# Rotary turns of a mixed-layer transformer block: the exchange of halves moves from a TensorE product to small DMAs

## The chip, the cores and the metric

The kernel runs on one core of a Trainium2 chip, as one program. The metric is the device time of one execution in microseconds (us), the median of three runs. The profile is of one execution, with the span from its first to its last instruction.

## The reference, cut to what matters

A sequence of 256 tokens with 1024 features goes through two stacks. The first has two layers, each a feed-forward network, a mixer and another feed-forward network. Mixer 0 has delta-rule heads and retention heads; mixer 1 has differential and dilated attention. The second stack has two more layers, each with block attention (8 heads of 64), a gated recurrence (hgrn, 4 heads) and attention to a memory. Queries and keys of retention, differential, dilated and block attention get a rotary turn:

```
x1, x2 = halves of the rotated dims
out = concat([x1 * cos - x2 * sin, x2 * cos + x1 * sin])
```

The halves are 32 of 64 dims for retention and differential attention, 64 of 128 for dilated attention. In block attention only the first 16 of 64 dims turn (8 and 8), and its queries and keys are normalised over 64 dims first.

## The kernel before, in words

Features lie on the partitions and tokens on the free axis, so that a half of a head is a range of partitions. A unit of rotary work is a 128-partition, 2-block, 256-token piece (128x512 f32). There are 18 units: `r64` 0 and 1 in mixer 0; `r64b` 0 to 3 and `r128` 0 to 3 in mixer 1; `mq0`, `mk0`, `mq1`, `mk1` (0 and 1 of each) in the two last mixers. All that multiplies weights is cut into panels of 1024 KB, loaded by SyncE's queue into three slots (`raw`), split by ScalarE into a high part (`w_hi`, L1571, in halves L1580) and by VectorE into a low part (`w_lo`, L1890, in halves L1873), and multiplied by TensorE in three products (L1060 to L1062). A panel can be multiplied as two halves.

The order of every engine is written out by hand as one list, `ORDER`, and each engine takes its own steps of it in that order. Lists of rounds are merged, and `weave` puts half panels between the rounds (`BESIDE_0`, `BESIDE_1`, `BESIDE_2`). Waits are on counted steps of other engines (`at(...)`).

One rotary unit is two steps:

```
swap (pe):  ps[:, bank] = matrix^T @ values          # L1454, a signed permutation, fp32
rope (dve): tmp = ps[:, bank] * sin                  # L2130
            values = values * cos                    # L2131
            values = values + tmp                    # L2132
```

Both are of the same round (`ROPE = [("pe","swap",0), ("dve","rope",0)]`). Around them:

- Mixer 0: the `beside` lists of `delta_rounds` hold the two swaps next to the doubling of a triangular inverse (`double_y`, `double`, `turn_again` on TensorE, L1317; `doubled` on VectorE, L2084; `corner` on GpSimd, L1029). `ret_scores` (L1428) waits for the second rope.
- Mixer 1: the four `r64b` units lie between panels 4 to 7 of `in1`; the four `r128` units, two per round, lie in the first two rounds of the attention heads. A head is `scores` (TensorE, L1478 and L1480), `mask_max` (VectorE, L2180), `exp` (ScalarE, L1784), `divide` (VectorE, L2193 to L2201), `turn_p` (TensorE, L1490), `p_cols` (ScalarE, L1795), `attend` (TensorE, L1433).
- Last mixers: after the last of eight `level` rounds of the recurrence (`k_level` on GpSimd, L1037), one normalisation per round: `cn_sq` (ScalarE), `cn_sum` (TensorE, L1465), `cn_rstd` (ScalarE, L1773 and L1774), `cn_use` (VectorE, L2144; for the `ho` units L2146, L2148, L2136, L2137), in the order mq 0, mk 0, mq 1, mk 1, ho 0, ho 1. The swap and rope of unit i lie in the round after its `cn_use`; a half panel lies in every round. Block attention starts seven rounds after the last level.

GpSimd has little to do: loads of tables (L1017), `add` (L1044), `corner`, `k_level`, and the four stores of the output (L1049).

Of the kernel before, what the change touches and what calls it, by code (L numbers as in the profile page):

```python
# [82 lines left out]
def tables():  # L83
# [6 lines left out]

    def swap(n, half, signs=True, width=None):

        m = np.zeros((P, P), f)
        for g in range(0, P, n):
            for d in range(half):
                m[g + d + half, g + d] = -1.0
                m[g + d, g + d + half] = 1.0
        return m

    def rope(dim):  # L100
        inv = (np.float32(10000.0) ** (-np.arange(0, dim, 2, dtype=f) / f(dim))).astype(f)
        ang = (np.arange(SEQ, dtype=f)[None, :] * inv[:, None]).astype(f)
        reps = P // (dim // 2)
        return np.tile(np.cos(ang), (reps, 1)).astype(f), np.tile(np.sin(ang), (reps, 1)).astype(f)

# [28 lines left out]
    for g in (0, 64):  # L134
        freq[g:g + half, 0] = inv2
        freq[g + half:g + 2 * half, 0] = inv2
# [3 lines left out]
        [("upper", upper), ("strict", strict_low), ("diag16", diag16), ("e16", below(16)), ("e32", below(32)),  # L140
         ("e64", below(64)), ("ret", np.concatenate(ret, axis=1)), ("cos64", cos64), ("sin64", sin64),
         ("swap64", swap(64, 32))],
        [("causal", causal), ("times", times), ("union", union), ("cos64", cos64), ("sin64", sin64),
         ("swap64", swap(64, 32)), ("cos128", cos128), ("sin128", sin128), ("swap128", swap(128, 64))],
        [("causal", causal), ("swapp", swap(64, 8)), ("levels", np.concatenate(levels, axis=1)),
         ("keep", keep), ("freq", freq)],
# [21 lines left out]
LATE = {name: (BASE[name] + N_OF[name] + SLOTS - 1, min(BASE[name] + N_OF[name] + SLOTS, PANELS)) for name in DOWNS}  # L168
UNCOUNTED = {"out_part", "half", "half_hi", "half_lo", "gate_first", "up_first", "first_hi", "first_lo", "ffn_down", "logs", "split_hi", "split_lo", "ffn", "panel", "load", "store"}
PAIRS = DC // 2  # L170
# [64 lines left out]
SCORES_FIRST = [ATTEND[1], ATTEND[0]] + ATTEND_TWO[2:]  # L235
ROPE = [("pe", "swap", 0), ("dve", "rope", 0)]
NORM_ROPE = NORM_COLS + [("pe", "swap", 2), ("dve", "rope", 2)]

# [107 lines left out]
def delta_rounds():  # L346
# [10 lines left out]
    for s in range(3):  # L357
        doubling += [both(("pe", "double_y", s), *([("pe", "turn_again", s)] if s else []), ("act", "y", s), *([("act", "t_again", s)] if s else [])),
                     both(("pe", "double", s), ("dve", "doubled", s), *([("pool", "corner", s + 1)] if s < 2 else []))]
    beside = [[("pe", "turn_v", (0,)), ("pe", "turn_v", (1,)), ("dve", "v_beta", (0,)), ("dve", "v_beta", (1,))],  # L360
              [("pe", "turn_k", ()), ("dve", "k_decayed", ()), ("pe", "swap", (("r64", 0),)), ("dve", "rope", (("r64", 0),))],
              [("pe", "swap", (("r64", 1),)), ("dve", "q_decayed", ()), ("dve", "rope", (("r64", 1),))],
              [(e, k, (h,)) for h in (0, 1) for e, k in (("pe", "ret_scores"), ("dve", "ret_decay"))],
# [61 lines left out]
def last_mixer(l):  # L425

    hgrn, ahead = hgrn_rounds(l)
    hgrn[ahead + 9] += [("act", "silu", (f"in2_{l}", 15)), ("act", "logs", ())]
    n = ahead + 9
    qk = [(f"mq{l}", 0), (f"mk{l}", 0), (f"mq{l}", 1), (f"mk{l}", 1)]  # L430
    h = n + 7
    chains = [hgrn,
              [[]] * n + rounds(NORM_COLS, qk + [(f"ho{l}", 0), (f"ho{l}", 1)]),
              [[]] * (n + 2) + rounds(ROPE, qk),
              [[]] * h + paired_heads(l),
              [[]] * (h + 6) + [[("dve", "gate_out", ((f"moba{l}", 0),))], [], [], [("dve", "gate_out", ((f"moba{l}", 1),))]],
              [[]] * (h + 13) + [y_splits(l, 0), y_splits(l, 2)]]
    if l == 0:
        load, *stats = mem_norm(1)
        chains += [[[]] * (h + 1) + [[load]]]  # L440
    if l:
        chains += [[[]] * (h + 7) + sum(([[("pe", "turn_back", (b,)), ("act", "rows_back", (b,))], []] for b in range(PAIRS)), [])]
    places = [n + r for r in BESIDE_2]
    if l:
        places[:4] = [0, 1, 2, 2]
    panels = panel_list(f"in2_{l}", None, 4)
    panels[-1] = [x for x in panels[-1] if x[1] != "evacuate"]
    out = weave(merge(*chains), halves(panels), places)
    return (out + late_splits(f"in2_{l}") + [("dve", "gate_out", ((f"matt{l}", g),)) for g in (0, 1)]
            + y_splits(l, 8) + y_splits(l, 10))  # L450
# [36 lines left out]
def order():  # L487
# [37 lines left out]
    out += weave(rounds(ROPE, [("r64b", g) for g in (0, 2, 1, 3)]), panel_list("in1", None, 4, 8), range(4))  # L525
    ropes = [[(e, k, (("r128", g),)) for g in pair for e, k, _ in ROPE] for pair in ((0, 2), (1, 3))]
    heads = rounds(SCORES_FIRST, [("dif", h) for h in range(4)] + [("dil", h) for h in range(4)])
# [56 lines left out]
def build(nc, x_in, mem_in, pos_in, panels, gains, small_in, tab0, tab1, tab2, tab3, out):  # L584
    with ExitStack() as ctx:
# [159 lines left out]
        def evac(name, k):  # L745
            return ("dve" if (name, k) in EVACUATED_BY_DVE else "act", "evacuate", name, k)

        ropes = {}
        for g in range(2):
            ropes["r64", g] = (rqk[:, 2 * g:2 * g + 2], tab(1, "swap64"), tab(1, "cos64"), tab(1, "sin64"), 3 - g, evac("in0", 11))  # L750
        for g in range(4):
            ropes["r128", g] = (cqk[:, 2 * g:2 * g + 2], tab(2, "swap128"), tab(2, "cos128"), tab(2, "sin128"), 6 + g // 2,
                                evac("in1", 4 + g))
            ropes["r64b", g] = (dqk[:, 2 * g:2 * g + 2], tab(2, "swap64"), tab(2, "cos64"), tab(2, "sin64"), 6 + g // 2,
                                evac("in1", g))
            for l in range(2):
                unit_ = ((f"mq{l}", f"mk{l}")[g // 2], g % 2)
                ropes[unit_] = (mo_qk[:, 2 * g:2 * g + 2], tab(3, "swapp"), cos_a, sin_a, 2 + g // 2, ("dve", "cn_use", unit_))
        rope_list = [a for e, k, a in ORDER if k == "swap"]
        rope_index = {a[0]: i for i, a in enumerate(rope_list)}  # L760

# [175 lines left out]
        last_use["mem0"] = ("dve", "cn_use", ("ro", 1))  # L937
        last_use["mem1"] = ("dve", "cn_use", ("ho0", 1))

# [70 lines left out]
        def _(pool):  # L1010
# [20 lines left out]
            def k_level(l, v):  # L1031
# [5 lines left out]
                nc.gpsimd.tensor_tensor(k_l[v % 2], k_g, dec_f[v % 2], ALU.mult).then_inc(pool_done, 1)  # L1037

            def add(tag, b):

# [11 lines left out]

            steps("pool", {"load": load, "add": add, "zero": zero, "corner": corner, "k_level": k_level, "store": store})


        @block.tensor
        def _(pe):
# [383 lines left out]

            def swap(unit):
                values, matrix, _, _, bank, ready = ropes[unit]
                pe.wait_ge(done[ready[0]], at(*ready))
                if rope_index[unit] >= 2:
                    pe.wait_ge(dve_done, at("dve", "rope", rope_list[rope_index[unit] - 2][0]))
                for t_ in ("tab1", "tab2", "tab3"):
                    if unit[0] in {"tab1": ("r64",), "tab2": ("r128", "r64b"), "tab3": ("mq0", "mk0", "mq1", "mk1")}[t_]:
                        pe.wait_ge(loaded[t_], 16)
                if unit[0] == "r64b":  # L1450
                    pe.wait_ge(dve_done, at("dve", "ropes_scaled"))
                if unit[0] == "r64":
                    pe.wait_ge(dve_done, at("dve", "k_decayed") if unit[1] else at("dve", "v_beta", 1))
                pe.matmul(ps[:, bank], matrix, values, start=True, stop=True).then_inc(pe_done, 1)  # L1454

            def cn_sum(unit):
# [79 lines left out]
            def hgrn_out(l, g):  # L1536
                pe.wait_ge(dve_done, at("dve", "level_in", l, 7))
                for i in range(2):
# [11 lines left out]
                         "from_state": from_state, "delta_out": delta_out, "ret_scores": ret_scores, "ret_out": ret_out,  # L1550
                         "swap": swap, "cn_sum": cn_sum, "scores": scores, "turn_p": turn_p, "attend": attend,
                         "lam_sum": lam_sum, "diagonal": diagonal, "level": level, "hgrn_out": hgrn_out})
# [291 lines left out]
        def _(dve):  # L1844
# [279 lines left out]
            def rope(unit):  # L2124
                values, _, cos, sin, bank, _ = ropes[unit]
                dve.wait_ge(pe_done, at("pe", "swap", unit))
                if unit[0][0] == "m":
                    dve.wait_ge(act_done, at("act", "sines"))
                tmp = grid(xn[:, 512:1024], 2)
                step(tt(tmp, grid(ps[:, bank], 2), spread(sin, 2), ALU.mult))  # L2130
                step(tt(values, values, spread(cos, 2), ALU.mult))  # L2131
                finish(tt(values, values, tmp, ALU.add))  # L2132
# [264 lines left out]
```

## Time and profile before

| | |
|---|---|
| time, median of 3 runs | 1557.71 us (1556.43 to 1557.83) |
| profiled execution: span | 1554.0 us |
| profiled execution: mean granted TensorE clock | 0.997 |
| TensorE busy | 1499.8 us, 97% |
| VectorE busy | 1171.7 us, 75% |
| ScalarE busy | 763.9 us, 49% |
| GpSimd busy | 94.1 us, 6% |
| DMA, mean | 159 GB/s, 246.76 MB |

The page gives the span of the profiled execution and no other time for it. The three runs took 2.4 to 3.8 us more than this span, the median 3.7 us more; a change of the span is taken as a change of the time. The busy shares are averages over stages that have different limits.

### The profile page before, as it was taken

How to read it: one execution, taken by the hardware profiler on the slowest of the kernel's cores; microseconds unless marked ns; L12 is line 12 of the kernel's file. 1: busy time of each engine (PE TensorE's matmuls, PEld its weight loads, DVE VectorE, ACT ScalarE, POOL GpSimd, SP SyncE). 2: the span in 40 equal slices, each digit the busy share in tenths (PEclk: the TensorE clock that was granted, in tenths of full speed). 3: DMA queues.
4: the chain of work that ended last, by engine and by line, in shares of the span. 5: the costliest groups of instructions: out<-in, count | busy, mean ns of one | idle time of the engine just before them, and what ended most of it. 6: DMA issues, size and time to landing. Idle time of an engine off the chain costs nothing.

```text
span 1554.0 us, 23910 instructions
## 1 busy us (share of the span) xinstructions
PE 1499.8 (97%) x9958; PEld 1343.8 (86%) x9958; DVE 1171.7 (75%) x1387; ACT 763.9 (49%) x935; POOL 94.1 (6%) x66
## 2 busy tenths in 40 slices
PE   7999999999999999999998899999999989999988
PEld 6888899988888888888887888888899869899967
DVE  7878668756887788787676688787779676579774
ACT  5333456445433453334445543345565675564662
POOL 2000010011000010000100100001113001003100
PEclk9999999999999999999999999999999999999999
DMA  7555535214655555555441365554344315444302
GB/s 272 209 190 189 170 131 188 82 55 159 213 189 199 179 178 190 190 185 194 163 163 56 134 216 190 192 188 175 151 163 152 109 42 189 175 149 152 120 28 81
DMA packets 51888, 246.76 MB, mean 159 GB/s; under 512 B 4619, under 2 KB 5771, under 8 KB 27718
## 3 DMA queue, kind: packets, MB, share of 16 engines
q1 hardware_dynamic: 50662, 238.29, 43.8%
q0 software_dynamic: 1120, 6.96, 1.2%
q8 instruction: 79, 1.29, 0.3%
q14 instruction: 27, 0.22, 0.0%
HBM read 244.18 MB, written 1.05 MB: 158 GB/s over the span
## 4 chain that ended last, share of the span: by engine, by line
PE 76%; DVE 13%; ACT 7%; issue 3%; DMA 0%; SPq 0%; DVEq 0%; ACTq 0%; POOL 0%
PE ps L1109 20%; PE ps L1111 10%; PE ps L1060 9%; PE ps L1062 9%; PE ps L1061 9%; PE ps L1162 8%; PE ps L1317 4%; PE ps L1163 4%; DVE w_lo L1890 3%; ACT w_hi L1571 2%; DVE act_two L1998 1%; PE ps L1465 1%; ACT work L1784 1%; ACT act_two L1649 1%; PE ps L1454 1%
## 5 line engine op out<-in xcount | busy, mean ns | idle before, releaser
L1571 ACT ACTIVATE w_hi<-raw 128x2048 fp32r<-128x2048 f32 x186 | 355.2, 1914 | 396.6 <-PE ps L1111 276.6
L1890 DVE TENSOR_TENSOR w_lo<-raw,w_hi 128x2048 fp32r<-128x2048 f32 x186 | 432.4, 2331 | 139.1 <-ACT w_hi L1571 136.3
L1109 PE MATMUL ps<-act_two,w_hi 128*128 128x512 f32 x1408 | 445.1, 398 | 5.0 <-DVE w_lo L1890 2.4
L1060 PE MATMUL ps<-act_two,w_hi 128*128 128x256 f32 x1120 | 329.0, 294 | 9.9 <-DVE act_two L1998 5.3
L1111 PEld LDWEIGHTS ps<-act_two,w_lo 128*128 128x128 f32 x1408 | 265.6, 189 | 63.1
L1061 PE MATMUL ps<-act_two,w_hi 128*128 128x256 f32 x1120 | 316.7, 283 | 0.0
L1062 PE MATMUL ps<-act_two,w_lo 128*128 128x256 f32 x1120 | 316.7, 283 | 0.0
L1111 PE MATMUL ps<-act_two,w_lo 128*128 128x256 f32 x1408 | 277.5, 279 | 0.0
L1060 PEld LDWEIGHTS ps<-act_two,w_hi 128*128 128x128 f32 x1120 | 214.6, 192 | 17.0 <-issue 6.1
L1109 PEld LDWEIGHTS ps<-act_two,w_hi 128*128 128x128 f32 x1408 | 215.5, 190 | 8.0 <-DVE w_lo L1890 3.6
L1061 PEld LDWEIGHTS ps<-act_two,w_hi 128*128 128x128 f32 x1120 | 214.7, 192 | 4.4 <-issue 4.3
L1062 PEld LDWEIGHTS ps<-act_two,w_lo 128*128 128x128 f32 x1120 | 214.5, 192 | 0.0
L1162 PE MATMUL ps<-g_two,w_hi 128*128 128x512 f32 x384 | 135.7, 396 | 0.0
L1873 DVE TENSOR_TENSOR w_lo<-raw,w_hi 128x1024 fp32r<-128x1024 f32 x76 | 103.5, 1388 | 27.4 <-ACT w_hi L1580 26.1
L1162 PE MATMUL ps<-act_two,w_hi 128*128 128x512 f32 x320 | 113.0, 397 | 2.5 <-DVE act_two L1929 2.5
L1163 PE MATMUL ps<-g_two,w_lo 128*128 128x256 f32 x384 | 107.2, 279 | 0.0
L1060 PE MATMUL ps<-w_hi,act_two 128*128 128x256 f32 (+1 forms) x336 | 105.0, 312 | 0.2 <-ACT work L1668 0.2
L1061 PE MATMUL ps<-w_lo,act_two 128*128 128x256 f32 (+1 forms) x336 | 100.1, 298 | 0.0
L1062 PE MATMUL ps<-w_hi,act_two 128*128 128x256 f32 (+1 forms) x336 | 100.1, 298 | 0.0
L1044 POOL TENSOR_TENSOR pair<-pair 128x512 f32<-128x512 f32 x27 | 41.2, 1526 | 858.7 <-ACT pair L1628 857.9
L1163 PE MATMUL ps<-act_two,w_lo 128*128 128x256 f32 x320 | 89.3, 279 | 0.0
L1162 PEld LDWEIGHTS ps<-g_two,w_hi 128*128 128x128 f32 x384 | 72.1, 188 | 16.7
(286 smaller groups left out, 1995.5 us busy)
## 6 DMA issues: line engine op xcount, KB each, us to landing
raw<-panels SPq DMA_DIRECT2D x184, 1024.0 KB, 4.8
raw<-panels SPq DMA_DIRECT2D x80, 512.0 KB, 4.9
raw<-panels SPq DMA_DIRECT2D x8, 256.0 KB, 5.7
table<-tab POOLq DMA_DIRECT2D x1, 1472.0 KB, 9.4
table<-tab POOLq DMA_DIRECT2D x1, 1216.0 KB, 5.5
xn<-x_in SPq DMA_DIRECT2D x4, 256.0 KB, 4.9
work<-mem_in POOLq DMA_DIRECT2D x1, 1024.0 KB, 9.3
xn<-mem_in POOLq DMA_DIRECT2D x1, 1024.0 KB, 6.3
```

Source lines behind the costliest of these rows:

```text
L1044: nc.gpsimd.tensor_tensor(pair[:, 0:512], pair[:, 0:512], pair[:, 512 * b:512 * b + 512], ALU.add).then_inc(pool_done, 1)
L1060: pe.matmul(o, l[0], r[0], start=start, stop=False, skip_group_check=shared)
L1061: pe.matmul(o, l[0], r[1], start=False, stop=False, skip_group_check=shared)
L1062: return pe.matmul(o, l[1], r[0], start=False, stop=stop, skip_group_check=shared)
L1109: pe.matmul(grid(ps[:, bank + half], 2), w[half][0], act_two[:, slots[c]], start=c == 0, stop=False)
L1111: ins = pe.matmul(ps[:, bank + half, 0:SEQ], w[half][1], act_hi[:, slots[c]], start=False, stop=c == DC - 1)
L1162: pe.matmul(grid(ps[:, bank], 2), hi, two, start=first and m == 0, stop=False)
L1163: ins = pe.matmul(ps[:, bank, 0:SEQ], lo, two[:, 0], start=False, stop=last and m == len(quarters) - 1)
L1317: ins = pe.transpose(oh, lhs(h), ident) if turn else pe.matmul(oh, lhs(h), rhs(h), start=True, stop=True)
L1571: nc.scalar.activation(w_hi[:, s], raw[:, s], ACT.Copy).then_inc(panel_hi, 1)
L1873: ins = tt(w_lo[:, s, c], raw[:, s, c], w_hi[:, s, c].bitcast(F32), ALU.subtract)
L1890: tt(w_lo[:, s], raw[:, s], w_hi[:, s].bitcast(F32), ALU.subtract).then_inc(panel_lo, 1)
```

## The change

The permutation product goes. In its place GpSimd's queue issues DMAs that copy, inside SBUF, each half of a head to the partitions of the other half, into a new buffer `other` (free parts of `work`). The sign goes into the sine table, whose first half of each head is negated; for block attention the frequency of the first 8 dims is negated. A unit of 64-wide heads takes 4 DMAs (of 32 partitions with 2 KB each, or of 8 partitions for block attention), a unit of 128-wide heads takes 2 of 64 partitions: 8 + 16 + 8 + 32 = 64 DMAs in all. Each unit has its own semaphore, and `rope` waits for all its DMAs. `rope` comes one round after the exchange in `ROPE`. In mixer 0 the exchanges are listed two rounds ahead at most, and the ropes stay where they were. In the first two rounds of the heads of mixer 1, all four `r128` exchanges are listed in the first round and the ropes in the second and third. In each last mixer a new step `still` zeroes the 128x2048 buffer, because only 16 of 64 rows per head are ever written there. The load of the second memory waits for the last rope.

```diff
-ROPE = [("pe", "swap", 0), ("dve", "rope", 0)]
+ROPE = [("pool", "swap", 0), ("dve", "rope", 1)]

 # delta_rounds
-    beside = [[("pe", "turn_v", (0,)), ("pe", "turn_v", (1,)), ("dve", "v_beta", (0,)), ("dve", "v_beta", (1,))],
-              [("pe", "turn_k", ()), ("dve", "k_decayed", ()), ("pe", "swap", (("r64", 0),)), ("dve", "rope", (("r64", 0),))],
-              [("pe", "swap", (("r64", 1),)), ("dve", "q_decayed", ()), ("dve", "rope", (("r64", 1),))],
+    beside = [[("pool", "swap", (("r64", 0),)), ("pool", "swap", (("r64", 1),)), ("pe", "turn_v", (0,)), ("pe", "turn_v", (1,)), ("dve", "v_beta", (0,)), ("dve", "v_beta", (1,))],
+              [("pe", "turn_k", ()), ("dve", "k_decayed", ()), ("dve", "rope", (("r64", 0),))],
+              [("dve", "q_decayed", ()), ("dve", "rope", (("r64", 1),))],

 # last_mixer
-              [[]] * (n + 2) + rounds(ROPE, qk),
+              [[]] * (n + 1) + [[("pool", "still", (l,))]] + rounds(ROPE, qk),

 # order
-    ropes = [[(e, k, (("r128", g),)) for g in pair for e, k, _ in ROPE] for pair in ((0, 2), (1, 3))]
+    ropes = [[("pool", "swap", (("r128", g),)) for g in (0, 2, 1, 3)]] + [[("dve", "rope", (("r128", g),)) for g in pair] for pair in ((0, 2), (1, 3))]

-        last_use["mem1"] = ("dve", "cn_use", ("ho0", 1))
+        last_use["mem1"] = ("dve", "rope", ("mk0", 1))

+            def still(l):
+                pool.wait_ge(pe_done, at("pe", "level", l, 7))
+                nc.gpsimd.memset(work[:, 5120:7168], 0.0).then_inc(pool_done, 1)
+
+            def swap(unit):
+                values, to, _, _, (n, half), ready = ropes[unit]
+                pool.wait_ge(done[ready[0]], at(*ready))
+                if unit[0] == "r64":
+                    pool.wait_ge(pe_done, at("pe", "pow8", 1))
+                if unit[0] == "r128":
+                    pool.wait_ge(dve_done, at("dve", "rope", ("r64b", unit[1])))
+                if unit[0][0] == "m":
+                    pool.wait_ge(pool_done, at("pool", "still", int(unit[0][2])))
+                for a in range(0, P, n):
+                    pool.dma_start(to[a:a + half], values[a + half:a + 2 * half]).then_inc(swapped[unit], 16)
+                    pool.dma_start(to[a + half:a + 2 * half], values[a:a + half]).then_inc(swapped[unit], 16)

             def rope(unit):
-                dve.wait_ge(pe_done, at("pe", "swap", unit))
+                dve.wait_ge(swapped[unit], 32 * P // n)
+                if unit[0] == "r64":
+                    dve.wait_ge(loaded["tab1"], 16)
...
-                step(tt(tmp, grid(ps[:, bank], 2), spread(sin, 2), ALU.mult))
+                step(tt(tmp, other_, spread(sin, 2), ALU.mult))
```

Here `ready` is the step that wrote the values: an evacuation, or `cn_use` in the last mixers. TensorE's `swap`, with its waits for bank use, for tables and for `ropes_scaled`, is removed, and the three permutation matrices leave the tables.

## Rows read from the trace of the kernel before

**Rows 1.** The page: TensorE's busy time, and the shares of the last chain.
```profile
PE 1499.8 (97%) x9958; PEld 1343.8 (86%) x9958; DVE 1171.7 (75%) x1387; ACT 763.9 (49%) x935; POOL 94.1 (6%) x66
...
PE 76%; DVE 13%; ACT 7%; issue 3%; DMA 0%; SPq 0%; DVEq 0%; ACTq 0%; POOL 0%
```

**Rows 2.** Groups by line of TensorE: busy us, mean ns, idle before.
```profile
L1454 PE MATMUL ps<-work,table 128*128 128x512 f32 x36 | 18.1, 594 | 0.4 <-DVE table L1992 0.4
```

**Rows 3.** The chain in mixer 0: start us, us.
```profile
317.27 0.86 PE ps L1454 x2
...
319.92 0.86 PE ps L1454 x2
```

**Rows 4.** Timeline of TensorE in mixer 0: start us, us, engine, line, operation.
```profile
304.09 1.06 PE L1317 MATMUL ps<-work,xn 128*128 128x128 f32 x8
...
326.24 0.71 PE L1428 MATMUL ps<-work 64*128 64x256 f32 x4
```

**Rows 5.** Timeline of VectorE in mixer 0.
```profile
324.03 0.69 DVE L2132 TENSOR_TENSOR work<-work,xn 128x512 f32<-128x512 f32 x1
```

**Rows 6.** Timeline of GpSimd, mixer 0 and the first of two last mixers.
```profile
316.09 2.50 POOL L1029 TENSOR_TENSOR work<-work,table 128x512 f32<-128x512 f32 x2 [13.08 <-PE ps L1317]
...
1196.48 2.43 POOL L1037 TENSOR_TENSOR xn<-work,pair 128x1024 f32<-128x1024 f32 x1 [5.12 <-ACT work L1671]
```

**Rows 7.** Timeline of VectorE: pairs of half-panel splits in two places.
```profile
351.50 2.36 DVE L1873 TENSOR_TENSOR w_lo<-raw,w_hi 128x1024 fp32r<-128x1024 f32 x2
...
1197.86 3.27 DVE L1873 TENSOR_TENSOR w_lo<-raw,w_hi 128x1024 fp32r<-128x1024 f32 x2
```

**Rows 8.** Timeline of TensorE in mixer 1.
```profile
798.71 1.02 PE L1454 MATMUL ps<-work,table 128*128 128x512 f32 x2
...
805.31 1.88 PE L1454 MATMUL ps<-work,table 128*128 128x512 f32 x4
...
828.86 0.50 PE L1478 MATMUL ps<-work 64*128 64x128 f32 x4 [1.47 <-DVE stat L2180]
```

**Rows 9.** The chain in mixer 1.
```profile
807.94 2.29 DVE w_lo L1890
...
819.35 0.70 DVE work L2132
...
821.31 1.88 ACT work L1784 x8
...
827.52 0.28 DVE work L2180
```

**Rows 10.** Timeline of TensorE in the first of the two last mixers.
```profile
1228.91 1.02 PE L1465 MATMUL ps<-pair,const 128*128 128x512 f32 x2
```

**Rows 11.** Timeline of VectorE in the same mixer.
```profile
1223.05 0.75 DVE L2144 SCALAR_TENSOR_TENSOR work<-work,small,pair 128x512 f32<-128x512 f32 x1 [3.34 <-ACT pair L1774]
...
1231.36 0.75 DVE L2144 SCALAR_TENSOR_TENSOR work<-work,small,pair 128x512 f32<-128x512 f32 x1 [0.40 <-ACT pair L1774]
...
1235.95 0.75 DVE L2144 SCALAR_TENSOR_TENSOR work<-work,small,pair 128x512 f32<-128x512 f32 x1 [0.40 <-ACT pair L1774]
```

**Rows 12.** The chain in the same mixer.
```profile
1240.54 0.76 DVE xn L2146
...
1247.39 0.70 DVE act_two L2137
```

**Rows 13.** Timeline of GpSimd: one of the four stores.
```profile
1548.76 0.54 POOL L1049 DMA_DIRECT2D out<-work  x1 [0.82 <-DVE work L1964]
```

**Rows 14.** The page, DMA issues: count, KB each, median us to landing.
```profile
table<-tab POOLq DMA_DIRECT2D x1, 1472.0 KB, 9.4
...
out<-work POOLq DMA_DIRECT2D x4, 256.0 KB, 2.5
```

**Rows 15.** Stretches of mixer 1: us, busy us (x count) of PE, PEld, DVE, ACT, POOL; clock; DMA.
```profile
850.00:852.00 2.00, 0.79 (x4) 0.55 (x4) 1.90 (x11) 1.56 (x6) 0.00 (x0) 1.00 0.04 8
...
854.00:856.00 2.00, 2.00 (x3) 0.76 (x3) 0.00 (x0) 0.30 (x1) 0.00 (x0) 0.51 0.00 0
```

More of the change, by code:

```diff
@@ L89, in tables @@
     strict_low = (part > free).astype(f)
[L91 to L98, printed above, removed]
     def rope(dim):
@@ L102, in rope @@
         ang = (np.arange(SEQ, dtype=f)[None, :] * inv[:, None]).astype(f)
-        reps = P // (dim // 2)
-        return np.tile(np.cos(ang), (reps, 1)).astype(f), np.tile(np.sin(ang), (reps, 1)).astype(f)
+        reps = P // dim
+        return np.tile(np.cos(ang), (2 * reps, 1)).astype(f), np.tile(np.concatenate([-np.sin(ang), np.sin(ang)]), (reps, 1)).astype(f)
     q0 = part - free
@@ L134, in tables @@
     for g in (0, 64):
-        freq[g:g + half, 0] = inv2
+        freq[g:g + half, 0] = -inv2
         freq[g + half:g + 2 * half, 0] = inv2
@@ L140, in tables @@
         [("upper", upper), ("strict", strict_low), ("diag16", diag16), ("e16", below(16)), ("e32", below(32)),
-         ("e64", below(64)), ("ret", np.concatenate(ret, axis=1)), ("cos64", cos64), ("sin64", sin64),
-         ("swap64", swap(64, 32))],
+         ("e64", below(64)), ("ret", np.concatenate(ret, axis=1)), ("cos64", cos64), ("sin64", sin64)],
         [("causal", causal), ("times", times), ("union", union), ("cos64", cos64), ("sin64", sin64),
-         ("swap64", swap(64, 32)), ("cos128", cos128), ("sin128", sin128), ("swap128", swap(128, 64))],
-        [("causal", causal), ("swapp", swap(64, 8)), ("levels", np.concatenate(levels, axis=1)),
+         ("cos128", cos128), ("sin128", sin128)],
+        [("causal", causal), ("levels", np.concatenate(levels, axis=1)),
          ("keep", keep), ("freq", freq)],
@@ L168 @@
 LATE = {name: (BASE[name] + N_OF[name] + SLOTS - 1, min(BASE[name] + N_OF[name] + SLOTS, PANELS)) for name in DOWNS}
-UNCOUNTED = {"out_part", "half", "half_hi", "half_lo", "gate_first", "up_first", "first_hi", "first_lo", "ffn_down", "logs", "split_hi", "split_lo", "ffn", "panel", "load", "store"}
+UNCOUNTED = {"swap", "out_part", "half", "half_hi", "half_lo", "gate_first", "up_first", "first_hi", "first_lo", "ffn_down", "logs", "split_hi", "split_lo", "ffn", "panel", "load", "store"}
 PAIRS = DC // 2
@@ L746, in evac @@
             return ("dve" if (name, k) in EVACUATED_BY_DVE else "act", "evacuate", name, k)
+        other = [region(1024 + 512 * i, 2, SEQ) for i in range(2)]
+        other_1 = [region(13312 + 512 * i, 2, SEQ) for i in range(4)]
+        other_2 = [region(5120 + 512 * i, 2, SEQ) for i in range(4)]
         ropes = {}
         for g in range(2):
-            ropes["r64", g] = (rqk[:, 2 * g:2 * g + 2], tab(1, "swap64"), tab(1, "cos64"), tab(1, "sin64"), 3 - g, evac("in0", 11))
+            ropes["r64", g] = (rqk[:, 2 * g:2 * g + 2], other[g], tab(1, "cos64"), tab(1, "sin64"), (64, 32), evac("in0", 11))
         for g in range(4):
[L752 to L755, printed above, removed]
+            ropes["r64b", g] = (dqk[:, 2 * g:2 * g + 2], other_1[g], tab(2, "cos64"), tab(2, "sin64"), (64, 32), evac("in1", g))
+            ropes["r128", g] = (cqk[:, 2 * g:2 * g + 2], other_1[g], tab(2, "cos128"), tab(2, "sin128"), (128, 64), evac("in1", 4 + g))
             for l in range(2):
                 unit_ = ((f"mq{l}", f"mk{l}")[g // 2], g % 2)
-                ropes[unit_] = (mo_qk[:, 2 * g:2 * g + 2], tab(3, "swapp"), cos_a, sin_a, 2 + g // 2, ("dve", "cn_use", unit_))
-        rope_list = [a for e, k, a in ORDER if k == "swap"]
-        rope_index = {a[0]: i for i, a in enumerate(rope_list)}
+                ropes[unit_] = (mo_qk[:, 2 * g:2 * g + 2], other_2[g], cos_a, sin_a, (64, 8), ("dve", "cn_use", unit_))
+        swapped = {u: sem("swapped_" + u[0] + f"_{u[1]}") for u in ropes}
         def bank_of(name, k):
@@ L1051, in store @@
                     pool.wait_ge(stored, 16 * TILES * 2)
-            steps("pool", {"load": load, "add": add, "zero": zero, "corner": corner, "k_level": k_level, "store": store})
+            steps("pool", {"load": load, "add": add, "still": still, "swap": swap, "zero": zero, "corner": corner, "k_level": k_level, "store": store})
         @block.tensor
@@ L1440, in ret_out @@
                          ret_p[h][:, 0:SEQ], ret_p[h][:, SEQ:384]).then_inc(pe_done, 1)
[L1442 to L1454, printed above, removed]
             def cn_sum(unit):
@@ L1550, in _ @@
                          "from_state": from_state, "delta_out": delta_out, "ret_scores": ret_scores, "ret_out": ret_out,
-                         "swap": swap, "cn_sum": cn_sum, "scores": scores, "turn_p": turn_p, "attend": attend,
+                         "cn_sum": cn_sum, "scores": scores, "turn_p": turn_p, "attend": attend,
                          "lam_sum": lam_sum, "diagonal": diagonal, "level": level, "hgrn_out": hgrn_out})
@@ L2124, in rope @@
             def rope(unit):
-                values, _, cos, sin, bank, _ = ropes[unit]
-                dve.wait_ge(pe_done, at("pe", "swap", unit))
+                values, other_, cos, sin, (n, _), _ = ropes[unit]
+                dve.wait_ge(swapped[unit], 32 * P // n)
+                if unit[0] == "r64":
+                    dve.wait_ge(loaded["tab1"], 16)
                 if unit[0][0] == "m":
```

1 line of the change is left out of this document (removed).

## The prediction

> **What bounds the kernel now.** I read the page first: TensorE is busy 97% of the span and the last chain runs on it for three quarters [rows 1]. So work taken off TensorE should count, but only where the chain is really there. Therefore I read, stage by stage, the groups by line for the price of the product, the chain in the four places with rotary units, and then the timelines of TensorE, VectorE and GpSimd, to see who is ready first once the product is gone. A difference of under 0.2% (3.1 us) can't be told from none here.
>
> The 18 products are 36 records [rows 2]; one product occupies TensorE and the chain for 0.86 us [rows 3]. All 18 together are 18 x 0.86 = 15.5 us. That is the most this change can give. I now go through the places and ask what is left of it.
>
> **Mixer 0 (2 units).** Both products are on the chain [rows 3], 1.72 us. The exchanges may be issued when TensorE has finished the records that end at 305.15 [rows 4], far ahead of the first rope at 318.1, and GpSimd is free until its corners at 316.09 [rows 6]. One issue of GpSimd takes 0.54 us [rows 13]; eight take 4.3 us and end at 309.5. The landing is not shown for such copies: the lower bound is the store's 2.5 us, the upper one the table's 9.4 us [rows 14]. Even the upper gives 309.0 + 9.4 = 318.4 for the second unit, which is needed only after 322. I price the exchange at nothing here; it is covered by the inverse's rounds. Now VectorE is late next. The retention scores start at 326.24 [rows 4] and would start at 324.5, but they wait for the second rope, whose last instruction ended at 324.72 [rows 5]. The rope no longer waits for its product, 0.15 us earlier. Against this, its first multiply will read two SBUF operands at 318.1, while GpSimd's corner runs from SBUF until 318.59 [rows 6]. The trace shows what that does: a pair of half splits takes 3.27 us where GpSimd's k_level overlaps it and 2.36 us elsewhere [rows 6, 7]. So the multiply starts at 318.6, the second rope ends at 325.1, and the scores start 1.1 us earlier than before instead of 1.72. Bounds: -1.6 (no blocking) and -1.1. I take -1.1, since the row shows the blocking. Taken on its own, "SBUF — State Buffer" (Who interferes with whom) in the Trainium skill says the same: a VectorE instruction with two SBUF inputs waits for a GpSimd one that reads SBUF, and does not wait for one that only writes. By this rule the new zeroing of the buffer would block nothing, and mixer 0 keeps the 1.1.
>
> **Mixer 1 (8 units).** The first four products lie between full panels, where TensorE is the chain: 4 x 0.86 = 3.44, plus the 0.4 us wait for the scaled tables before the first [rows 2], is 3.9 us. The exchanges of these units can all go as soon as their panels are evacuated, a panel or more ahead; covered. From 805.31 the other four products [rows 8] come. But the chain leaves TensorE there: the split of 807.94, two pairs of ropes with a mask_max behind each, then ScalarE's exp, a split, and the next mask_max at 827.52 [rows 9]. TensorE waits 1.47 us for VectorE at 828.86 [rows 8]. After the change VectorE's order is split, mask_max, ropes, mask_max, then exp and the splits on both engines, then the second pair of ropes, then the third mask_max. These are the same pieces in series; only their order differs. So the four products at 805 and 813 give nothing back, and the stage keeps 3.9 us. The r128 exchanges are issued from about 796 and the last at 803, against ropes at 807.5 and 819: covered even by 9.4 us.
>
> **Last mixers (4 units each).** Before, a round was 4.59 us: a sum, a product and a half panel on TensorE. VectorE's work in it (cn_use, rope, half split) is 4.59 - 0.40 = 4.19 us [rows 11]. Take the product out and TensorE's round is 3.73 us, shorter than VectorE's: VectorE becomes the bound. Walk it through with the rope one round later:
> - The cn_use of mq 1 comes 2.45 us after the start of its sum [rows 10, 11]. One product fewer stands before it: 1231.36 - 0.86 = 1230.50. Its round now has the rope of mq 0: until 1230.50 + 4.22 = 1234.72.
> - The next cn_use is ready at 1235.95 - 1.72 = 1234.23, so VectorE is already the later one: until 1238.94.
> - The cn_use of ho 0 was at 1240.54 and is ready at 1240.54 - 2.58 = 1237.96; it starts at 1238.94, 1.6 us earlier than before.
> - Before, VectorE then did cn_use, one rope, cn_use, until 1248.1 [rows 12], 7.58 us. Now there are two ropes in this tail, because of the lag. A rope is three instructions of 0.69 [rows 5], with gaps 2.18 us. So 1238.94 + 7.58 + 2.18 = 1248.7.
> - The first mask_max of block attention stands behind that on VectorE, and exp, divide and turn_p behind mask_max. It is 0.6 us later than before, though TensorE arrives 3.4 us earlier.
>
> So each last mixer costs 0.6 us instead of giving 3.4. The second has the same rounds. The zeroing starts at 1215 and must be done by 1223.8, when the first exchange is ready: a 128x1024 product takes GpSimd 2.43 us [rows 6], so twice that, 4.9, is my upper bound and 0 the lower; covered by 8.8 us. What waits behind the exchanges on GpSimd is the load of the second memory, 0.6 us later, needed some 30 us on.
>
> The exchange itself has less cover here. The one of mq 0 is issued from 1223.80 [rows 11]; the fourth DMA starts 3 x 0.54 = 1.6 us later; VectorE comes for it at 1230.50 + 0.78 = 1231.3. The landing may thus take 5.9 us before it costs anything; the other three have more. Bounds: 1.6 + 2.5 (no wait) and 1.6 + 9.4 = 11.0 us (3.5 us wait in each mixer). I take the store's 2.5 us: its 256 KB from SBUF by the same queue is nearer to 16 KB pieces than a 1472 KB table. A page alone has a price for this: by "DMA: Bandwidth & Descriptors" (Anatomy of one DMA) of the Trainium skill a small DMA of this path takes about 2.0 us, most of it the receipt of the write; an estimate with it would leave the sum as it is.
>
> **The sum.** -1.1 - 3.9 + 0.6 + 0.6 = -3.8 us. The span 1554.0 becomes 1550.2. The median of the runs stands 3.7 us above the span, so 1553.9 us. The extra traffic is 3.1 MB of 247; I leave it out.
>
> **Rivals.**
> - *Everything given to TensorE is kept.* Speaks for it: 97% busy. Against: the chain is on VectorE in the heads and in the tails [rows 9, 12]. It would give 1557.7 - 15.5 = 1542.2.
> - *Late landings.* If a copy lands late because it shares the engines with panel loads, VectorE stands at the first rope of each last mixer. At 9.4 us it costs 3.5 each: 1560.9; halfway, 1557.4. For it: the only heavily mixed row. Against: its size.
> - *The clock falls.* In mixer 1, VectorE's share does not shrink, so TensorE will wait in one piece: its work from 801.4 ends near 819, the next scores come at 828.86 - 3.9 = 825, 6 us idle. In the last mixers it would stand 3 us before the scores of the second pair. The trace has one fall, to half (1.2 GHz), after a stretch in which TensorE was busy 0.8 us of 2 [rows 15]; sums on the chain took twice 0.86 there and attention products 0.43 more, 1.3 us in all. Three such falls on the chain take back 3.9: 1557.8. Against: in mixer 1 the slowed half panel has slack. In the Trainium skill, "TensorE: Matmul & The Clock Gate" (The HAM clock gate) states that idling halves the clock; by this rule it would fall, and the trace agrees that it can.
> - *Slower: the software queue takes the copies one after another.* Place: the last mixers, where 16 DMAs are issued from 1223.8 and the last must be there by 1246.5. It decides from 1.63 us per DMA (26.2 us for 16, 3.5 us late in each mixer, over 3.1 us slower in all). At 2.5 us each, 40 us: 17.3 late twice and 2.3 in mixer 0, about 1591. Against: the stores were issued 1.4 us apart, each landing after 2.5, so two were under way together [rows 13, 14].
>
> **How the numbers follow.** Forecast 0.54, with 1551.5 to 1556.5 as its own range (a clock fall more or less is 1.3 each way, mixer 0 up to 0.5). Everything kept 0.05, late landings 0.17, clock 0.15, one after another 0.09. The range 1550.5 to 1560.5 leaves out the first and the last of the rivals and the tips of the others. Faster: three quarters of 0.54, the 0.05, and 0.04 of the middle ones, 0.50. Slower: 0.09 and 0.04 of late landings, 0.13. Same: 0.37.
>
> **What would show it.** Mixer 0: retention scores about 1.1 us closer to the last corner, and the first rope's multiply longer than 0.69. Mixer 1: panels 4 to 7 at 5.75 us each, then an idle TensorE of some 6 us before the scores of the fourth head. Last mixers: half panels every 3.73 us, VectorE without idle time from the third cn_use on, and TensorE idle before the second pair of scores. I am wrong if ropes wait for DMAs, if an issue takes GpSimd much more than 0.54 us, or if VectorE's instructions are longer while GpSimd issues.

## The result and the profile after

| | before | after |
|---|---|---|
| time, median of 5 runs each (of before, the three runs above and two more) | 1556.43 us (1555.55 to 1557.83) | 1561.79 us (1560.98 to 1563.57) |
| span of the profiled execution | 1554.0 us | 1561.0 us |
| mean granted TensorE clock | 0.997 | 0.987 |

Ratio after to before 1.0034, 95% interval 1.0023 to 1.0045: the change makes the kernel 5.4 us slower. The forecast was 1553.9 us, with 1560.5 as the upper end of its range; it gave 0.13 to a kernel that is slower by more than 3.1 us.

To find where the time went I took marks, that is instructions of GpSimd that stand in both traces: the first corner of mixer 0, the load of the next table that ends a mixer, the first and last `add` of a norm, the load of the second memory, the stores. The table gives how much the distance between two marks grew, after minus before, in us:

| stage | forecast | measured |
|---|---|---|
| start, to the first `add` | 0 | +1.5 |
| mixer 0 (first corner to table load) | -1.1 | +2.25 |
| mixer 1 | -3.9 | -3.60 |
| last mixer 1 | +0.6 | +0.96 |
| last mixer 2 | +0.6 | +0.83 |
| last store's issue to the end of the span | 0 | +4.98 |

The stretches between these stages changed by 0.1 us in all. The start stands before any changed instruction; in the profiles of this study it lies between 16.8 and 19.1 us with and without the exchange, and the profiled execution is the slowest of the five. I leave it out. The other rows add up to +5.4 us, the difference of the medians. That they agree so closely is in part luck, since mixer 1 alone differs by 1.4 us between profiles of the same work (spare_counters, below).

**Mixer 0.** Timeline of TensorE after (start us, us); it answers to the scores of [rows 4]:

```profile
325.59 0.60 PE L1325 MATMUL ps<-const,work 128*128 128x128 f32 x4
328.50 0.83 PE L1436 MATMUL ps<-work 64*128 64x256 f32 x4 [2.31 <-DVE work L2128]
329.10 0.65 PE L1437 MATMUL ps<-work 64*128 64x128 f32 x4
329.69 3.32 PE L1325 MATMUL ps<-work,xn 128*128 128x128 f32 x16
```

TensorE stands 2.31 us in front of the retention scores, for the last instruction of the second rope. Timelines of VectorE and of GpSimd in the same place, against [rows 5, 6]:

```profile
318.98 0.69 DVE L2060 TENSOR_TENSOR work<-ps,stat 128x512 f32<-128x512 f32 x1 [4.19 <-PE ps L1325]
319.70 1.04 DVE L2126 TENSOR_TENSOR xn<-work,table 128x512 f32<-128x512 f32 x1
...
324.40 0.69 DVE L2126 TENSOR_TENSOR xn<-work,table 128x512 f32<-128x512 f32 x1
325.13 1.65 DVE L2127 TENSOR_TENSOR work<-work,table 128x512 f32<-128x512 f32 x1
326.81 1.63 DVE L2128 TENSOR_TENSOR work<-work,xn 128x512 f32<-128x512 f32 x1
```

```profile
317.70 2.50 POOL L1018 TENSOR_TENSOR work<-work,table 128x512 f32<-128x512 f32 x2 [6.33 <-PE ps L1325]
...
324.57 3.33 POOL L1018 TENSOR_TENSOR work<-work,table 128x512 f32<-128x512 f32 x2 [4.37 <-PE ps L1325]
```

Two instructions of the second rope take 1.65 and 1.63 us instead of 0.69 while the second pair of corners (324.57 to 327.90) runs on GpSimd. Beside the first pair it is the same: the rope's first multiply, with two SBUF operands, takes 1.04, while the one at 318.98, which reads PSUM, takes its usual 0.69. The second pair before, on GpSimd's timeline:

```profile
324.69 2.60 POOL L1029 TENSOR_TENSOR work<-work,table 128x512 f32<-128x512 f32 x2 [6.10 <-PE ps L1317]
```

It took 2.60 us, now 3.33, and it began just as the second rope ended at 324.72 [rows 5]. The stage begins 1.60 us later in the profile after. Measured from its start, TensorE delivers the pair's inputs 1.72 us sooner, with both products gone, while VectorE comes to the second rope 0.22 us later (324.40 against 322.58), so that the two now meet.

The wait has a tail. Stretches of the same time (us; busy us of PE, PEld, DVE, ACT, POOL; granted clock; DMA):

```profile
326.00:328.00 2.00, 0.19 (x2) 0.00 (x0) 1.97 (x2) 0.88 (x2) 1.90 (x2) 1.00 0.00 0
...
330.00:332.00 2.00, 2.00 (x11) 2.00 (x11) 1.09 (x3) 0.00 (x0) 0.00 (x0) 0.50 0.00 0
```

After the idle stretch the granted clock is 0.50, the lower level of 1.2 GHz. From the first score (328.50) to the next panel piece (333.79) TensorE takes 5.29 us for what took 3.70 before (326.24 to 329.94), 1.6 us more. "TensorE: Matmul & The Clock Gate" (The HAM clock gate) in the Trainium skill says that idling lowers the clock; the trace agrees. Sum: two products -1.72; without them the scores were due at 326.24 + 1.60 (shift of the stage) - 1.72 = 326.12 and came at 328.50, +2.38; the slow clock +1.59; together +2.25.

**Mixer 1.** Timeline of TensorE after, against 828.86 of [rows 8]:

```profile
828.73 0.59 PE L1472 MATMUL ps<-work 64*128 64x128 f32 x2 [5.63 <-DVE stat L2176]
```

This is the forecast's picture: TensorE is done early and waits some 6 us for the `mask_max` behind the second pair of ropes.

**Last mixers.** The chain after in the first of them, against [rows 12]:

```profile
1224.72 0.86 PE ps L1459 x2
...
1228.45 0.87 PE ps L1459 x2
...
1230.73 0.76 DVE work L2140
...
1234.84 0.75 DVE work L2140
...
1239.02 0.67 DVE xn L2142
...
1241.63 0.70 DVE xn L2126
...
1243.81 0.76 DVE xn L2142
...
1246.51 0.70 DVE xn L2126
...
1248.98 0.34 DVE work L2176
```

TensorE's rounds are 3.73 us, VectorE's 4.1 to 4.2, and two ropes stand in the tail, as walked through. The chain names no DMA. Before, the same `mask_max` stood in the chain at

```profile
1248.41 0.34 DVE work L2180
```

Less the 0.25 us by which this stage begins later, it is 0.32 us later. The other 0.64 us come behind it. Among them is a wait of VectorE for a product of TensorE, 0.43 us in front of the `mask_max` at 1253.48, where before (1252.56) there was none. The stretches there:

```profile
1247.00:1249.00 2.00, 0.00 (x0) 0.00 (x0) 1.90 (x6) 0.00 (x0) 0.06 (x1) 1.00 0.00 0
...
1251.00:1253.00 2.00, 1.82 (x7) 1.00 (x6) 1.56 (x8) 1.79 (x5) 0.00 (x0) 0.50 0.93 393
```

The second of them before, with the clock at its upper level:

```profile
1251.00:1253.00 2.00, 0.99 (x7) 0.52 (x6) 1.79 (x10) 1.91 (x4) 0.00 (x0) 1.00 0.93 381
```

**The exchanges themselves** are cheap. From the list of DMA issues (KB each, median us to landing) and the timeline of GpSimd (one issue):

```profile
work<-work POOLq DMA_DIRECT2D x24, 64.0 KB, 2.3
...
work<-work POOLq DMA_DIRECT2D x8, 128.0 KB, 3.7
...
work<-work POOLq DMA_DIRECT2D x32, 16.0 KB, 1.9
```

```profile
308.92 0.50 POOL L1045 DMA_DIRECT2D work<-work  x1
```

**The end.** The last store, before and after, on GpSimd's timeline:

```profile
1550.12 0.54 POOL L1049 DMA_DIRECT2D out<-work  x1 [0.82 <-DVE work L1964]
...
1552.14 0.54 POOL L1057 DMA_DIRECT2D out<-work  x1 [0.82 <-DVE work L1958]
```

The last store is issued 2.02 us later than before, but the span ends 8.9 us behind it (1561.0) instead of 3.9 (1554.0). The stores land no later. No engine shows an instruction there. TensorE stands still, and from about 1555 us on its granted clock is 0.50, so that a part of the lower mean clock in the table above is this idle end and costs nothing.

### The profile page after: what moved, and what is told of

Read it like the earlier page. It is cut to its first block, busy times and chain, and to the rows that moved or that the text cites. A ratio compares the mean times of both kernels' runs of the same rounds, so it can differ in the third digit from the quotient of the medians.

```text
span 1561.0 us, 23895 instructions
## 1 busy us (share of the span) xinstructions
PE 1495.5 (96%) x9922; PEld 1345.7 (86%) x9922; DVE 1173.4 (75%) x1387; ACT 764.5 (49%) x935; POOL 130.5 (8%) x132
## 4 chain that ended last, share of the span: by engine, by line
PE 75%; DVE 15%; ACT 6%; issue 2%; DMA 0%; SPq 0%; DVEq 0%; POOL 0%; ACTq 0%
PE ps L1117 20%; PE ps L1119 10%; PE ps L1068 9%; PE ps L1070 9%; PE ps L1069 9%; PE ps L1170 8%; PE ps L1171 4%; PE ps L1325 4%; DVE w_lo L1884 3%; ACT w_hi L1565 2%; DVE act_two L1992 1%; PE ps L1459 1%; ACT act_two L1643 1%; DVE w_lo L1867 1%; DVE work L2127 1%
```

## The experiments

Each kernel below is the changed kernel or the kernel before with the edit that is shown, cut to the lines that matter. Theory 1: in mixer 0 a collision of VectorE and GpSimd makes TensorE wait and the clock fall. For the end (the stretch from the last store's issue to the end of the span, 3.9 us before) there were two theories: A, each further semaphore lengthens it; B, each DMA of GpSimd's software queue does. Times are medians, ratios are to the kernel before in the same series, with 95% intervals. Its median was 1557.1 us for the first four kernels, 1556.8 for the next four, 1555.4 for the last two.

### m0_early: mixer 0's ropes where VectorE is idle

```
-  ... ("dve", "v_beta", (1,))],
-  [("pe", "turn_k", ()), ("dve", "k_decayed", ()), ("dve", "rope", (("r64", 0),))],
-  [("dve", "q_decayed", ()), ("dve", "rope", (("r64", 1),))],
+  ... ("dve", "v_beta", (1,)), ("dve", "rope", (("r64", 0),)), ("dve", "rope", (("r64", 1),))],
+  [("pe", "turn_k", ()), ("dve", "k_decayed", ())],
+  [("dve", "q_decayed", ())],
```

> The changed kernel with one thing moved: VectorE does both ropes of mixer 0 right behind v_beta, where it stood idle from 314.8 to 318.98 after the change, instead of after k_decayed and q_decayed. Theory 1 (the second rope collides with GpSimd's corner at 324.57, TensorE then waits 2.3 us and the clock falls to half for 3.4 us, 1.7 us lost): the retention scores no longer wait for a rope, no fall of the clock at 328, the stage from the first corner's inputs to the end of mixer 0 is 2.3 + 1.7 = 4.0 us shorter than in the changed kernel, the time about 1557.8. Rival (the exchange's DMAs are what makes the stage longer, by slowing others or by landing late): the stage changes by less than 1 us, about 1561.5.

Measured: 1557.63 us, ratio 1.0004 (0.9995 to 1.0012), 4.2 us below the changed kernel as the same series has it (1561.82, four_counters). Mixer 0 is 1.71 us shorter than before, 3.96 us shorter than in the changed kernel. Its VectorE timeline shows that the collision has only moved, to the first pair of corners, which start at 315.50:

```profile
315.54 1.78 DVE L2128 TENSOR_TENSOR work<-work,table 128x512 f32<-128x512 f32 x1
317.36 1.64 DVE L2129 TENSOR_TENSOR work<-work,xn 128x512 f32<-128x512 f32 x1
```

There it costs nothing: the rope ends at 319.0, TensorE needs it at 324, and the granted clock stays 1.00:

```profile
328.00:330.00 2.00, 2.00 (x20) 2.00 (x18) 0.90 (x2) 0.00 (x0) 0.00 (x0) 1.00 0.00 0
```

Theory 1 stands. The wait and the fall of the clock went together, so this run gives their sum and the timeline above how it divides. The rival of theory 1, that the exchange's own DMAs make mixer 0 longer, falls: they are all there.

### four_counters: 4 semaphores instead of 18

```
-swapped = {u: sem("swapped_" + u[0] + f"_{u[1]}") for u in ropes}
+slots = [sem(f"swapped_{i}") for i in range(4)]      # counted up from place to place
...
-dve.wait_ge(swapped[unit], 32 * P // n)
+dve.wait_ge(swapped[unit], full[unit])
```

> The changed kernel with 4 semaphores for the landings of the exchanges, counted up from place to place, instead of 18; the same 64 DMAs. The end of the changed kernel, from the last store's issue to the end of the span, is 8.9 us against 3.9 before. Theory A (each further semaphore lengthens the end, 5.0 / 18 = 0.28 us each): the end becomes 3.9 + 4 x 0.28 = 5.0 us and the time falls by 3 to 4 us, to about 1558. Theory B (the use of GpSimd's software queue, 64 more DMAs, lengthens the end): it stays at 8.9 us, and the time at 1561.8.

Measured: 1561.82 us, ratio 1.0028 (1.0018 to 1.0038); the end is 8.9 us. Against theory A.

### spare_counters: 18 idle semaphores in the kernel before

```
+spare = [sem(f"spare_{i}") for i in range(18)]
```

> The kernel before with 18 more semaphores that nothing uses, no exchange at all. Theory A, if it is their mere number that counts at the end: the end of the span 5.0 us longer, the time about 1556.4 + 4 = 1560. Theory B, or if only used ones count: no change, 1556.4.

Measured: 1556.20 us, ratio 0.9996 (0.9987 to 1.0005); the end is 3.8 us. Theory A is out. The profile is also a measure of noise: with the same work, mixer 1 is 1.4 us shorter and the stretch behind it 2.3 us longer than in the profile of before. The stretches show what goes with it. In the profile of before the granted clock falls at 852 to 856 us [rows 15], 14 us ahead of the end of mixer 1; here it stays 1.00 until 858 and falls at 858 to 862, 4 us ahead of that end. All profiles divide so. With the products mixer 1 takes 114.1 or 114.2 us where a fall lies at this earlier place (before, small_copies) and 112.65 where it does not (spare_counters). With the exchange it takes 110.2 to 110.5 us with the earlier fall (after, four_counters, mixer1_sync_queue, products_in_last, all_sync) and 108.7 with a later one or none (m0_early, early_lag0, only_mixer1, mixed_queues). Like against like, the exchange makes mixer 1 3.6 to 4.0 us shorter.

### only_mixer1: the exchange in mixer 1 alone

```
+by_product = ("r64", "mq0", "mk0", "mq1", "mk1")
...
+if unit[0] in by_product:
+    dve.wait_ge(pe_done, at("pe", "half_turn", unit))   # the product of before
+    other_ = grid(ps[:, turn[unit][2]], 2)
```

> The exchange in mixer 1 alone (8 units, 24 DMAs, 8 semaphores); mixer 0 and the last mixers keep the permutation product on TensorE and the order of before. Mixer 1 gives back 3.6 us as in the changed kernel, the other stages are those of before. By theory A the end costs 8 x 0.28 = 2.2 us of span: 1556.4 - 3.6 + 2 = about 1555. By theory B it costs 5.0 x 24/64 = 1.9 if it goes with the number of DMAs, or the whole if one is enough: 1555 to 1558. If the gain of mixer 1 hung on the other places it would be 1556.4 or more.

Measured: 1553.94 us, ratio 0.9979 (0.9970 to 0.9988): 3.1 us below before. In its profile mixer 0 and the last mixers are those of before within 0.04 us, and the end is 1.76 us longer for 24 DMAs. So mixer 1 gives 3.1 + 1.8 = 4.9 us; with the interval's 1.4 us to either side this agrees with the 3.9 forecast, and it does so without the other places. The profile by itself has mixer 1 5.42 us shorter than before and the stretch behind it 2.31 us longer; against spare_counters, whose fall of the clock comes late too, the two are 3.98 us shorter and 0.03 us longer.

### small_copies: 64 copies that nobody needs, in the kernel before

```
 pool.dma_start(to, of_).then_inc(loaded[tag], 16)
+if tag == "tab1":
+    for i in range(64):
+        pool.dma_start(scrap[...], const[...]).then_inc(small_copies, 16)     # 32 partitions x 64 bytes
```

> The kernel before, with all its products, and 64 small copies (32 partitions x 64 bytes) issued on GpSimd's queue right behind the first table's load at 24 us, into a tile that nothing reads; GpSimd is idle there until 194 us. Theory B (each software DMA, whenever it is issued, lengthens the end of the program): the last stage's times stay, the end of the span after the last store's issue goes from 3.9 to 8.9 us, the time from 1557.1 to about 1561. Rival: the longer end comes from something else in the changed kernel (semaphores are already out), then the end stays 3.9 us and the time 1557.1.

Measured: 1561.89 us, ratio 1.0033 (1.0021 to 1.0046), as slow as the changed kernel. The copies are issued here, where GpSimd is idle:

```profile
25.41 31.59 POOL L1022 DMA_DIRECT2D scrap<-const  x64
```

The mixers are unchanged, all within 0.1 us. The last store and the span:

```profile
1549.82 0.54 POOL L1054 DMA_DIRECT2D out<-work  x1 [0.82 <-DVE work L1970]
```

```profile
span 1559.0 us, 23976 instructions
```

From the store to the end it is 9.2 us, 5.3 more than before, for DMAs that were issued over 1490 us earlier. Theory B stands.

### mixer1_sync_queue: the same exchange, issued by SyncE

```
 for n in range(2, PANELS):
     load_panel(n)
+    for unit in after_load.get(n, []):   # r64b g behind panel g + 6 of in1, r128 g behind panel g + 9
+        exchange(unit)
```

> The kernel with the exchange in mixer 1 alone, but its 24 DMAs issued by SyncE between the panel loads (each unit's copies behind the load that comes 6 or 5 panels after the unit's own panel) instead of by GpSimd. Theory B (the end is paid per DMA of GpSimd's software queue): the end is 3.9 us again instead of 5.6, mixer 1 keeps its gain, the time is 1.8 us below that kernel's 1553.9, about 1552.2. Rival (any DMA more lengthens the end): 1553.9. Risk: a copy issued late makes a rope wait, or delays a panel's load; then mixer 1 is longer by what TensorE waits.

Measured: 1551.84 us, ratio 0.9974 (0.9962 to 0.9985). Mixer 1 is 3.8 us shorter than before, and the end is 3.7 us long. It is DMAs of GpSimd's queue that lengthen the end, not DMAs as such. The copies land later on this queue, in a median of 4.7 us (64 KB) and 4.0 us (128 KB), but no rope waits for one.

### early_lag0: in the last mixers, the rope one round sooner

```
-ROPE = [("pool", "swap", 0), ("dve", "rope", 1)]
+... rounds([("pool", "swap", 0), ("dve", "rope", 0)], qk)      # last mixers only; with m0_early
```

> The changed kernel with mixer 0's ropes early (1557.6) and, in the last mixers, each rope in the same round as its unit's cn_use instead of one round later; the exchange is issued right behind the cn_use and VectorE has only a half split to do before the rope. From the rows of the changed kernel: four issues of 0.5 us and a landing of 1.9 us after the cn_use, so 3.9 us, of which a split covers 0.8 to 1.2: VectorE waits about 2.7 us in each of four rounds, and rounds of 4.19 + 2.7 = 6.9 us replace 4.1. If the lag is worth its tail, this one is slower: 4 x 2.7 - 2.2 = 8.6 us in each last mixer at most, about 1570. If the lag's extra rope in the tail is the larger cost, it is faster than 1557.6.

Measured: 1555.87 us, ratio 0.9996 (0.9987 to 1.0005), 1.8 us below m0_early where I had expected up to 12 more. My expectation had misread the order: the round of a rope already is the one behind its `cn_use`, so the next unit's `cn_use` stands between them even without the lag. In the first of the last mixers VectorE waits twice only (the profile names the `cn_use` just done; what `rope` waits for in the code is the exchange's DMAs):

```profile
1226.11 0.69 DVE L2127 TENSOR_TENSOR xn<-work,table 128x512 f32<-128x512 f32 x1 [0.20 <-DVE work L2141]
...
1230.96 0.69 DVE L2127 TENSOR_TENSOR xn<-work,table 128x512 f32<-128x512 f32 x1 [0.79 <-DVE work L2141]
```

In the second it waits 0.96 us (1460.99, for a DMA) and 1.26 us (1470.42), 2.2 us together. Against m0_early, which has the lag, the first mixer is 1.35 us shorter and the second 0.15 us. One rope fewer in the tail (2.2 us) thus pays for 1.0 us of waiting in the first and just about for 2.2 us in the second. The two last mixers together are 0.6 us longer than before, with the lag 2.1.

### products_in_last: exchange in mixers 0 and 1, products in the last mixers

```
-[[]] * (n + 1) + [[("pool", "still", (l,))]] + rounds([("pool", "swap", 0), ("dve", "rope", 1)], qk),
+[[]] * (n + 2) + rounds([("pe", "half_turn", 0), ("dve", "rope", 0)], qk),      # with m0_early and four_counters
```

> The exchange in mixer 0 (ropes early) and in mixer 1, the products of before in the last mixers, landings on 4 semaphores: 32 DMAs on GpSimd's queue. By stages: mixer 0 -1.7, mixer 1 -3.9, last mixers 0, end 32 x 5.0/64 = 2.5 us of span: 3.1 us below before, 1554.0. Against the changed kernel with early ropes (1557.6) it takes out 0.95 + 0.83 of the last mixers and 2.5 of the end, 4.3 us. If the last mixers were not slower for the exchange, only the 2.5 would come: 1555.1.

Measured: 1553.35 us, ratio 0.9977 (0.9967 to 0.9987), 4.3 us below m0_early. Mixer 0 -1.7, mixer 1 -3.6, last mixers 0, end +2.45 for 32 DMAs. The edit takes the zeroing and the rope's lag out of the last mixers together with the exchange, so the three are not told apart there.

### all_sync and mixed_queues: what the results point to

all_sync has the edits of m0_early, mixer1_sync_queue and products_in_last, and the exchanges of mixer 0 issued by SyncE behind the load of panel 15 counted from `in0`. mixed_queues leaves those 8 DMAs to GpSimd.

```
-after_load = {}
+after_load = {BASE["in0"] + 15: [("r64", 0), ("r64", 1)]}      # all_sync only
```

> The version that the results point to: exchange in mixer 0 (ropes early, behind v_beta) and in mixer 1, all 32 DMAs issued by SyncE, products in the last mixers. Mixer 0 -1.7, mixer 1 -3.9, end 0: 5.6 us below before, about 1551.2, ratio 0.9964. If the stages' gains do not add up, it is no better than the kernel with mixer 1 alone on SyncE (1551.8, ratio 0.9974).

> The same, but the 8 DMAs of mixer 0 issued by GpSimd, the 24 of mixer 1 by SyncE. If the end is paid per DMA of GpSimd's queue, it is 8 x 5.0/64 = 0.6 us longer than 3.9, and the time 0.6 us above the other. If one such DMA between the table loads is enough for the whole, 5.0 us.

Measured: all_sync 1549.49 us, ratio 0.9962 (0.9950 to 0.9974), 5.9 us faster than before. mixed_queues 1551.00 us, ratio 0.9969 (0.9959 to 0.9979); its end is 0.45 us longer than before, all_sync's 0.17 us shorter. By stages all_sync has mixer 0 -1.71 and mixer 1 -3.89, as expected. The intervals of the two overlap, so that the 0.6 us between their ends rest on the profiles.

The end of the span behind the last store's issue, in all profiles:

| DMAs of GpSimd's queue more than before | kernels | end, us more than before | per DMA |
|---|---|---|---|
| 0 | spare_counters, mixer1_sync_queue, all_sync | -0.05, -0.22, -0.17 | |
| 8 | mixed_queues | 0.45 | 0.06 |
| 24 | only_mixer1 | 1.76 | 0.07 |
| 32 | products_in_last | 2.45 | 0.08 |
| 64 | after, m0_early, four_counters, early_lag0 | 4.98 to 5.04 | 0.08 |
| 64 of 2 KB | small_copies | 5.30 | 0.08 |

## Why the prediction was wrong

The steps that failed are two: in mixer 0 it let the second rope end on time beside a corner that its own sum had moved (-1.1 us, measured +2.25), and it counted nothing for what 64 more DMAs of GpSimd's queue cost at the end of the program (0, measured +4.98).

- **Mixer 0 (-1.1 forecast, +2.25 measured): the step failed.** It rightly saw that a rope from SBUF is blocked by a corner, and counted 0.5 us for it at the first corner; measured are 0.35, 1.04 us instead of 0.69. But it asked only what overlaps the rope in the trace of before. It let the second rope keep its place against the second corner, although its own sum moved the corner forward by 1.72 us, to 323.0, in the middle of the rope at 323 to 325. The rule of the Trainium skill that it cited ("SBUF — State Buffer", Who interferes with whom) covers this corner too, and the trace agrees: the two instructions that are long beside it read two SBUF operands.
- **The clock.** The fall was a rival with 1.3 us a time. In mixer 0 it was not considered, since no wait was expected; it took 1.6 us there, and m0_early, without the wait, has no fall. After the idle stretches of mixer 1 and of both last mixers the clock fell as well, for 6.7 to 6.8 us each, but no more than 0.6 us of the time of each last mixer can be put down to it. The prediction also says that the trace of before has one fall; there is a second, at 26 to 30 us in the start, which changes nothing here.
- **Mixer 1 (-3.9, measured -3.6): right**, with the 6 us of idle TensorE (5.63) and without a fresh wait. The slowed work behind it has slack, as the prediction said. Over all profiles, like against like, the stage gives 3.6 to 4.0 us.
- **Last mixers (+0.6 each, measured +0.96 and +0.83): right in mechanism,** VectorE the bound and a rope more in the tail; the tail itself measured +0.32, and the 0.64 behind it come where the clock is at half. That these 0.64 are the clock's is argued from the rows, not tried by itself. products_in_last shows that the loss comes with the exchange, its zeroing and its lag: without them both are 0.
- **The exchange's landing and issue: right.** 1.9 and 2.3 us to landing for 16 KB and 64 KB against the 2.5 taken; the eight copies of 128 KB in mixer 1 took 3.7, which their cover held. An issue takes 0.50 us. The rivals of late landings and of a queue that serves one after another fell. None of the three signs of being wrong that the prediction named came, because it had looked for trouble in the exchange and not behind it.
- **Around the span (+3.7).** The sum set the span of one execution against the median of other executions. Where both are known of the same execution, the time is some 2.0 us above the span (medians of 1.85 to 2.07 in the later runs). It made the forecast too high, not too low, by 1.7 us.
- **The end: a term that was missing altogether,** 5.0 us, the largest. Nothing in the trace of before shows it, because that kernel has 11 such DMAs and no second kernel with another number stood beside it. The prediction priced a DMA by its issue and its landing alone.

Without the collision and its clock fall (4.0), and without the end (5.0), the changed kernel would be at about 1552.8, inside the range of the forecast's own case. The two were found apart: m0_early takes out the first, mixer1_sync_queue the second for mixer 1.

What stays open: what the chip does in the added 5 us, since no record lies there; and whether the cost goes by DMA or by its packets. The bytes do not matter, since 64 copies of 2 KB cost 5.3 us. The packets rose with the DMAs in every kernel, by 32 to 37 for each; small_copies has fewer of them than the changed kernel (2048 against 2176 more than before) and the longer end, which speaks for the DMAs, if weakly. Open too is what sets the place of the last fall of the clock in mixer 1.

## What to carry to other kernels

When work leaves an engine, everything that it released comes earlier: list which instructions of two other engines will meet anew, and not only those that overlap now. VectorE work with both operands in SBUF is worth putting where GpSimd is idle or where nobody waits for it. Small copies belong on a hardware queue (SyncE's) if its order has room, because each on GpSimd's queue costs some 0.08 us at the end of the program, however early it ran. And a product on TensorE costs little where VectorE's chain ends later, as behind the heads of mixer 1 and in the tails of the last mixers: replacing it there gained nothing. Before comparing a stage between two profiles, see whether both have the same falls of the clock in it.

## What the runs showed of the hardware

- A DMA from GpSimd's queue lengthens the end of the program by 0.06 to 0.08 us, whether it copies 2 KB at 25 us or 64 KB in mixer 1; 64 make 5.0 to 5.3 us. Semaphores, used (18 to 4) or idle (18 more), change the end by under 0.1 us.
- A VectorE multiply or add (128x512) that reads two SBUF operands and starts while a pair of GpSimd products runs, with over 1 us of the pair to go, takes 1.63 to 1.78 us instead of 0.69, and the pair of GpSimd products 2.95 to 3.33 instead of 2.5 to 2.6: both sides lose. The one that starts in the pair's last 0.5 us takes 1.04, and one that reads PSUM keeps its 0.69.
- 32 SBUF-to-SBUF copies of 16 KB, 16 in each last mixer, land in a median of 1.9 us each; within a unit they are issued 0.50 us apart, so that several are under way at once.
- After 2.31 us without a TensorE instruction the granted clock is at 0.50, and what took TensorE 3.70 us takes 5.29.
